# Expert rows through slot tables in DRAM in place of one-hot matmuls

## What is computed

```python
def moe_swiglu(x, router_w, router_b, w_gate_up, w_down):
    logits = x @ router_w + router_b                  # 256 tokens, 8 experts
    top_v, top_i = lax.top_k(logits, 2)
    gates = softmax(top_v)
    combine = sum(gates * one_hot(top_i))
    y = 0
    for e in range(8):                                # d_ff of an expert: 3584
        y = y + combine[:, e] * swiglu(x, w_gate_up[e], w_down[e])
    return y
```

## Time and profile before

| | us |
|---|---|
| median of 3 runs (2133.47 to 2137.73) | 2133.87 |
| profiled execution, first to last instruction | 2123.7 |
| TensorE matmul busy | 1955.9 (92%) |
| VectorE busy | 1397.3 (66%) |
| ScalarE busy | 1145.9 (54%) |
| GpSimd busy | 58.8 (3%) |
| mean granted TensorE clock | 0.924 |

### The profile page before, as it was taken

The page is one execution under the profiler, slowest core; times in us unless marked ns, Lnnn a source line. Parts: engine busy times, 40 slices in busy tenths (PEclk is TensorE's granted clock), DMA queues, the critical chain, the costliest instruction groups (busy, mean ns, idle before and its releaser), DMA issues.

```text
span 2123.7 us, 25981 instructions
## 1 busy us (share of the span) xinstructions
PE 1955.9 (92%) x9673; PEld 1625.0 (77%) x9673; DVE 1397.3 (66%) x1154; ACT 1145.9 (54%) x1009; POOL 58.8 (3%) x81
## 2 busy tenths in 40 slices
PE   7967999898889998877899999999999999999997
PEld 6756997685569986676687888878788787788875
DVE  3444775432254455454787888878888787888874
ACT  4333554343434333332576776767677776677762
POOL 1230000200000000000000000000000000000000
PEclk9958999896679999957799999999999999999997
DMA  6603455440034554401598999999999999899980
GB/s 227 197 30 138 158 193 185 141 165 21 0 134 169 197 178 159 139 1 60 204 363 310 351 350 334 351 321 358 341 334 348 331 354 332 316 352 337 362 296 35
DMA packets 251586, 486.86 MB, mean 229 GB/s; under 512 B 14108, under 2 KB 19292, under 8 KB 251536
## 3 DMA queue, kind: packets, MB, share of 16 engines
q1 hardware_dynamic: 244976, 477.30, 63.8%
q0 software_dynamic: 6560, 8.91, 1.4%
HBM read 484.05 MB, written 1.05 MB: 228 GB/s over the span
## 4 chain that ended last, share of the span: by engine, by line
PE 60%; DVE 13%; DMA 12%; ACT 8%; issue 4%; DVEq 2%; ACTq 0%; SPq 0%; POOL 0%; POOLq 0%
DMA w_raw<-in_moe_w_down 8%; PE psum L1759 8%; PE psum L1761 7%; PE psum L1760 7%; DVE w_lo L834 7%; PE psum L1416 7%; PE psum L1417 7%; PE psum L1418 6%; ACT w_hi L512 5%; DMA w_raw<-in_moe_w_gate_up 4%; PE psum L1447 3%; PE psum L1434 2%; PE psum L1437 2%; PE psum L1436 2%; PE psum L1802 1%
## 5 line engine op out<-in xcount | busy, mean ns | idle before, releaser
L834 DVE TENSOR_TENSOR w_lo<-w_raw,w_hi 128x2048 fp32r<-128x2048 f32 (+2 forms) x475 | 1031.7, 2200 | 384.1 <-ACT w_hi L512 381.1
L512 ACT ACTIVATE w_hi<-w_raw 128x2048 fp32r<-128x2048 f32 (+2 forms) x475 | 863.8, 1842 | 269.4 <-DMA w_raw<-in_moe_w_gate_up 103.8
L1759 PE MATMUL psum<-w_hi,xg_hi 128*128 128x512 f32 x896 | 360.3, 402 | 1.3 <-DVE w_lo L834 0.8
L1761 PE MATMUL psum<-w_hi,xg_lo 128*128 128x512 f32 x896 | 354.9, 396 | 0.0
L1760 PE MATMUL psum<-w_lo,xg_hi 128*128 128x512 f32 x896 | 354.8, 396 | 0.0
L1434 PE MATMUL psum<-xt_hi,w_hi 128*128 128x256 f32 x704 | 198.6, 282 | 3.8 <-DVE w_lo L834 2.1
L1761 PEld LDWEIGHTS psum<-w_hi,xg_lo 128*128 128x128 f32 x896 | 168.7, 188 | 41.0
L1759 PEld LDWEIGHTS psum<-w_hi,xg_hi 128*128 128x128 f32 x896 | 169.0, 189 | 40.2 <-DVE w_lo L834 1.7
L1760 PEld LDWEIGHTS psum<-w_lo,xg_hi 128*128 128x128 f32 x896 | 169.1, 189 | 38.0
L1436 PE MATMUL psum<-xt_lo,w_hi 128*128 128x256 f32 x704 | 197.9, 281 | 0.0
L1437 PE MATMUL psum<-xt_hi,w_lo 128*128 128x256 f32 x704 | 197.7, 281 | 0.0
(11 more groups left out here) (336 smaller groups left out, 2104.6 us busy)
## 6 DMA issues: line engine op xcount, KB each, us to landing
w_raw<-in_moe_w_gate_up SPq DMA_DIRECT2D x224, 1024.0 KB, 6.7
w_raw<-in_moe_w_down SPq DMA_DIRECT2D x96, 1024.0 KB, 6.7
w_raw<-in_w_up SPq DMA_DIRECT2D x22, 1024.0 KB, 5.7
w_raw<-in_ffn_w_gate_up SPq DMA_DIRECT2D x22, 1024.0 KB, 5.5
w_raw<-in_moe_w_down SPq DMA_DIRECT2D x32, 512.0 KB, 4.3
w_raw<-in_w_in SPq DMA_DIRECT2D x12, 1024.0 KB, 6.3
w_raw<-in_ab_w_in SPq DMA_DIRECT2D x12, 1024.0 KB, 5.4
w_raw<-in_w_down SPq DMA_DIRECT2D x10, 1024.0 KB, 6.5
```

The lines of the kernel that those rows point to most:

```text
L512: return act.activation(o, i, func, **kw)
L834: TT(w_lo[:, k % RING, 0:n], w_raw[:, k % RING, 0:n], w_hi[:, k % RING, 0:n].bitcast(F32), ALU.subtract)\
L1759: mm(o, hi[:, q, :], wh, start=(q == first), stop=False)
L1761: m = mm(o, lo[:, q, :], wh, start=False, stop=(q == last))
```

## The change

Tokens' rows go through tables in DRAM. At the start GpSimd fills x_slots (12 items of 128 rows) and the last three items of y_slots with zeros. After routing, each token has two slot numbers, one per chosen expert, and four indirect DMAs scatter the rows of x to x_slots. For each item SP loads its 128 rows (x_row), TensorE transposes them, and xg_hi and xg_lo are formed from that. The result is stored without the gate to y_slots by a DMA that ScalarE issues. At the end four indirect DMAs fetch each token's two rows, and VectorE adds them with the gates. The one-hot matmuls, sel, selt, xn_hi, xn_lo and ys_lo are gone.

```diff
+        (x_row, ys) = layout(at_xt, ("x_row", [P, D], F32), ("ys", [P, D], F32))
+        x_slots = nc.dram_tensor("x_slots", (ITEMS + 1, P, D), F32, kind="Internal").ap()
+        y_slots = nc.dram_tensor("y_slots", (ITEMS, P, D), F32, kind="Internal").ap()
# SP
+                def slot_rows(i):
+                    sp.wait_ge(S("x_scattered"), 16 * 2 * NT)
+                    sp.wait_ge(S("x_turned"), i)
+                    sp.dma_start(x_row[:], x_slots[bass.ds(i, 1)].rearrange("o p n -> (o p) n")).then_inc(S("x_row_landed"), 16)
...
+                        if j == MOE_PAIRS - 2:
+                            slot_rows(i + 1)
# GpSimd, after tri_ready
+                one(pool.memset(e2[:], 0.0))
+                for rows in [x_slots[i] for i in range(ITEMS + 1)] + [y_slots[i] for i in range(N_EXP, ITEMS)]:
+                    pool.dma_start(rows, e2[:].rearrange("p f n -> p (f n)")).then_inc(S("slots_zeroed"), 16)
# GpSimd, last
+                pool.wait_ge(S("slots_zeroed"), 16 * N_ZEROED)
+                pool.wait_ge(S("slot_ids"), 1)
+                for t in range(NT):
+                    for k in range(2):
+                        pool.indirect_dma_start(out=rows(x_slots), out_offset=row_of(t, k), in_=x[:, t, :], in_offset=None)\
+                            .then_inc(S("x_scattered"), 16)
+                pool.wait_ge(S("x_scattered"), 16 * 2 * NT)
+                pool.dma_start(x_row[:], x_slots[0]).then_inc(S("x_row0_landed"), 16)
+                pool.wait_ge(S("y_stored"), 1)
+                for t in range(NT):
+                    for k in range(2):
+                        pool.indirect_dma_start(out=y_row[:, t, k, :], out_offset=None, in_=rows(y_slots), in_offset=row_of(t, k))\
+                            .then_inc(S(f"y_landed{t}"), 16)
# ScalarE, start of the program, before the second exponential of cum
+            act.wait_ge(S("slots_zeroed"), 16 * N_ZEROED)
# ScalarE, end of an item (k is chunk 34 after take_item; 44 to 47 are the next item's 0 to 3)
+                rounds(k, k + 2, r)
+                take_item(i + 1)
+                k += 2
                 for n in range(2):
                     end = MOE_UP_CHUNKS + len(MOE_DOWN) * (n + 1)
                     rounds(k, end + 2, r)
                     k = end + 2
                     wait_used(act, c0 + end, r)
-                    copy(ys_hi[:, n * NB:(n + 1) * NB], psum[:, 4 + n, :], scale=gslot[:, 0:1])\
-                        .then_inc(S("ys_hi_ready"), 1)
-                take_item(i + 1, k, r)
+                    copy(ys[:, n * NB:(n + 1) * NB], psum[:, 4 + n, :]).then_inc(S("ys_ready"), 1)
+                act.wait_ge(S("ys_ready"), 2 * i + 4)
+                act.dma_start(y_slots[bass.ds(i, 1)].rearrange("o p n -> (o p) n"), ys[:]).then_inc(S("ys_landed"), 16)
+                rounds(k, k + 1, r)
+                act.wait_ge(S("ys_landed"), 16 * i + 16)
+                rounds(k + 1, k + 2, r)
# VectorE, end of an item
-                for n in range(2):
...
-                    STT(ys_lo[:, o], psum[:, 4 + n, :], gslot[:, 0:1], ys_hi[:, o].bitcast(F32), ALU.mult, ALU.subtract)\
-                        .then_inc(S("ys_ready"), 1)
+                splits(k, k + 2, r)
                 take_item(i + 1)
-                for t in range(NT):
-                    dve.wait_ge(S("scattered"), 2 * i + t + 1)
-                    TT(y[:, t, :], y[:, t, :], psum[:, 4 * t:4 * t + 2, :].rearrange("p b n -> p (b n)"), ALU.add)\
-                        .then_inc(S("y_added"), 1)
-                splits(k, k + 2, r)
+                splits(k + 2, MOE_CHUNKS + 4, r)
# VectorE, take_item
-                dve.tensor_copy(xg_lo[:], psum[:, 2:4, :].rearrange("p b (k n) -> p (b k) n", n=P)).then_inc(S("xg_ready"), 1)
+                dve.wait_ge(S("xg_hi_ready"), n + 1)
+                TT(xg_lo[:], psum[:, 2:4, :].rearrange("p b (k n) -> p (b k) n", n=P), xg_hi[:].bitcast(F32), ALU.subtract)\
+                    .then_inc(S("xg_ready"), 1)
# VectorE, after the last item
                 for t in range(NT):
+                    dve.wait_ge(S(f"y_landed{t}"), 32)
+                    for k, g in enumerate((g1, g2)):
+                        STT(y[:, t, :], y_row[:, t, k, :], g[:, t:t + 1], y[:, t, :], ALU.mult, ALU.add)
+                        dve.drain()
# TensorE
-            def gather(part, b0):
...
-            def turn_sel(n):
...
+            def turn_x(n):
+                for k in range(KD):
+                    m = turn(psum[:, 2 + k // 4, (k % 4) * P:(k % 4 + 1) * P], x_row[:, k * P:(k + 1) * P])
+                m.then_inc(S("x_turned"), 1)
...
                         if k == MOE_UP_CHUNKS:
                             turn_h(MOE_PAIRS - 1)
+                            pe.wait_ge(S("x_row_landed"), 16 * i + 16)
+                            turn_x(i + 1)
...
-                pe.wait_ge(S("sel_ready"), i + 2)
-                gather(xn_hi, 6)
-                gather(xn_lo, 2)
-                pe.wait_ge(S("ys_ready"), 2 * i + 2)
-                for t in range(NT):
-                    for n in range(2):
-                        for q, part in enumerate((ys_hi, ys_lo)):
-                            m = mm(psum[:, 4 * t + n, :], selt[:, t * P:(t + 1) * P], part[:, n * NB:(n + 1) * NB],
-                                   start=(q == 0), stop=(q == 1))
-                    m.then_inc(S("scattered"), 1)
-                turn_sel(i + 1)
# TensorE, before item 0
-                pe.wait_ge(S("sel_ready"), 1)
                 pe.wait_ge(S("ppt_ready"), 2)
-                gather(xn_hi, 6)
-                gather(xn_lo, 2)
-                turn_sel(0)
+                pe.wait_ge(S("x_row0_landed"), 16)
+                turn_x(0)
```

More of the change, by code:

```diff
@@ L766, in rounds, with take_item @@
                     round_chunk(N_BEFORE_MOE + k, r, item_width(k))
[L768 to L775, removed]
+            def take_item(n):
+                act.wait_ge(S("x_turned"), n + 1)
+                copy(xg_hi[:], psum[:, 2:4, :].rearrange("p b (k n) -> p (b k) n", n=P)).then_inc(S("xg_hi_ready"), 1)
             def item(i):
@@ L1326, in _ @@
                 dve.drain().then_inc(S("chosen"), 1)
+                dve.wait_ge(S("ranks"), 1)
+                ranks = scr[:, 1, 0:NT * N_EXP].rearrange("p (t e) -> p t e", e=N_EXP)
+                of_tiles = lambda v: v.unsqueeze(1).broadcast_to([P, NT, N_EXP])
+                TS(over, scr[:, 1, 16:24], float(P), None, ALU.is_gt)
+                TS(past, ranks, float(P), None, ALU.is_ge)
+                TT(slot_of, ranks, of_tiles(first8), ALU.add)
+                dve.drain()
+                dve.tensor_tensor_scan(over_upto, one8, over, 0.0, ALU.mult, ALU.add)
@@ new lines, in _ @@
+                dve.reduce_sum(eidf[:, 3:4], over, AX_X)
+                dve.drain()
+                STT(past8, over_upto, float(P), past8, ALU.mult, ALU.add)
+                TS(route_i[:, 3:4], eidf[:, 3:4], float(N_EXP), None, ALU.add).then_inc(S("counted"), 1)
+                dve.drain()
+                TT(past, past, of_tiles(past8), ALU.mult)
+                dve.drain()
+                TT(slot_of, slot_of, past, ALU.add)
+                dve.drain()
+                for k, (on, hot) in enumerate(((on1, hot1), (on2, hot2))):
+                    TT(on, slot_of, hot, ALU.mult)
@@ L1329, in _ @@
+                dve.drain()
+                for k, on in enumerate((on1, on2)):
+                    dve.reduce_sum(slotf[:, k, :], on, AX_X)
+                dve.drain()
+                dve.tensor_copy(slot_id[:], route[:, 228:232])
+                dve.drain().then_inc(S("slot_ids"), 1)
+                splits(2, 4, 0)
                 dve.wait_ge(S("top_exp"), 1)
-                dve.wait_ge(S("ranks"), 1)
-                sc, cc_ = (v.rearrange("p (t i) -> p t i", i=ITEMS) for v in (slotc[:, 0:NT * ITEMS], combc[:, 0:NT * ITEMS]))
@@ L1341, in _ @@
                 TT(g2, g1, gap_e, ALU.mult)
-                dve.tensor_tensor_scan(over_before, one8, over, 0.0, ALU.mult, ALU.add)
-                dve.reduce_sum(eidf[:, 3:4], over, AX_X)
-                dve.drain()
-                for hot, g in ((hot1, g1), (hot2, g2)):
-                    TT(hot, hot, g.unsqueeze(2).broadcast_to([P, NT, N_EXP]), ALU.mult)
-                dve.drain()
-                TT(comb, hot1, hot2, ALU.add)
-                TT(cc_[:, :, 0:N_EXP], hot1, hot2, ALU.add)
@@ L1351, in _ @@
-                dve.drain()
-                select(0)
-                TS(route_i[:, 3:4], eidf[:, 3:4], float(N_EXP), None, ALU.add).then_inc(S("counted"), 1)
-                TT(over_before, over_before, over, ALU.subtract)
-                take_item(0)
-                splits(2, 4, 0)
-                dve.drain()
                 for k in range(ITEMS - N_EXP):
-                    TS(pick, over_before, float(k), None, ALU.is_equal)
+                    TS(pick, tmp8, float(k), None, ALU.is_equal)
```

103 lines of the change are left out of this document (32 added, 71 removed).

## The result

| | before | after |
|---|---|---|
| median (us) | 2133.67 (2124.96 to 2137.73, 4 runs) | 2152.2 (2151.34 to 2152.84, 4 runs) |
| span of the profiled execution | 2123.7 | 2150.3 |
| after to before, all runs taken together, 95% interval | | 1.0096 [1.0068, 1.0123] |

The change made the kernel 18.5 us slower by the medians, 0.9%; the interval leaves out 1, so the loss is clear of the spread of the runs. The forecast was 2125 (2100 to 2150), faster: the sign was wrong and the time fell 2 us outside the range.

The account below looks back on a forecast made before the run. TensorE was taken to bound the inside of an item. Expert stage -23.8 us, ahead of item 0 +10.3 and behind the last item +4.5 gave -9.0, from 2133.9 to 2125 us (8-in-10 range 2100 to 2150).

Parts of the forecast that it names:

- the term for the boundary: Between two items: TensorE waits 0.8 us at chunk 0 and 1.3 before chunk 3, 2.1 per boundary (0.8 to 4.5).
- the lower clock ahead of item 0: Before the first expert matmul: eight transposes at the lower clock, 2.0 us; first matmuls 0.79 us in either kernel.
- The ring's term: Inside items: 1.05 MB more through the DMA engines costs 1.0 us per item (nothing to 2.7), 8 us in all.
- the stage: First to last expert matmul, eight items: 1032.8 us before, 1009.0 after, a change of -23.8 us.
- Ahead of item 0: Ranks to first expert matmul: slot numbers, four scatters, landing, x_row load, transposes; +10.3 us (+4 to +23).
- a sign of being wrong: Ahead of item 0: scatter issues above 2 us on GpSimd would show the forecast wrong; 1.2 us each was taken.
- Two covers of the prediction: Ahead of item 0: picking experts for second items is hidden under the scatters; without that cover some 6 us.
- Behind the last item: Last down matmul to statistics of y: store, indirect gathers and additions take 25.7 us against 21.2, +4.5 (-0.5 to +16).
- At the start: Fifteen zero writes (7.9 MB) on GpSimd's idle queue cost nothing; up to 20 us without that cover.
- The clean boundary: Rival: store lands in 2.8 us, each boundary costs 0.8, the ring takes the extra bytes; 2108 us, chance 0.20.
- The ring as the bound: Rival: the weight ring bounds the items, at 349 GB/s an item takes 129.2 us; total 2149 us, chance 0.16.
- The slow chain: Rival: GpSimd issues of 2.1 us and landings of 9.2, ahead of and behind the items; +15, 2149 us, chance 0.17.

Follow-up runs that it names:

- the moved wait: Changed kernel with ScalarE's wait for the ys store moved to just before the copy that overwrites ys, an item later: 2116.36 us, ratio 0.9937.
- the three runs on one chip: Changed kernel with the ys wait moved; without the ys store and wait; also without x_row loads for items 1 to 7: 2116.36, 2110.6, 2114.8 us.
- all kernels with a moved wait: Seven kernels on three chips with all the traffic and the ys wait moved an item later, some with further edits: items 125.1 to 126.3 us, mean 125.8.
- the three kernels of the first chip: Changed kernel with the ys wait moved; without the ys store and wait; also without x_row loads for items 1 to 7: ratios 0.9937, 0.9917, 0.993.
- the half store: Changed kernel, wait left in place, ys stored in two halves, each as soon as it is copied: 2145.07 us, ratio 1.0095.

## Why the prediction was wrong

**The step that failed is the term for the boundary: "With a landing time L ... It stalls L - 3.0 ... I take 4.3, since the store too shares the engines with two loads."** L is 7.0, above even the upper end of 6.7. With it the formula gives 4.0 + 0.8 = 4.8 us per boundary and the trace shows 4.6 (3.5 before chunk 3 and 1.1 before chunk 0). Mechanism and formula held; the size was taken from the nearest row by bytes (a 512 KB load between loads), when the nearest by position would have been the 6.7 us of the 1 MB loads that run with it. That is 2.5 us times seven, 18 us. Its bytes weren't the reason: the store's own packets take 2.7 us, and more than half of the landing passes before the first of them. The Trainium skill (DMA: Bandwidth & Descriptors, Anatomy of one DMA), cited in the prediction for 3.2 us, is further off; it gives the figure for transfers that GpSimd issues. The same section of the Trainium skill puts most of a transfer's fixed part into the receipt behind the last byte; these traces differ, with 3.6 to 4.1 us ahead of the first packet and 0.3 to 0.5 us between the last packet and the landing.

**What was not counted is the clock.** Windows of 10 us behind four stalls, and one across the start of an item:

```profile
1183.10:1193.10 10.00, 10.00 (x36) 7.94 (x37) 8.64 (x5) 6.85 (x4) 0.00 (x0) 0.83 0.85 290
...
1311.38:1321.38 10.00, 10.00 (x31) 7.99 (x32) 8.63 (x5) 6.85 (x4) 0.00 (x0) 0.70 0.83 288
...
1441.94:1451.94 10.00, 9.35 (x41) 7.33 (x42) 8.63 (x5) 7.16 (x5) 0.00 (x0) 1.00 0.83 282
...
1703.19:1713.19 10.00, 10.00 (x37) 7.96 (x38) 8.64 (x5) 6.86 (x4) 0.00 (x0) 0.84 0.86 292
...
1952.45:1962.40 9.95, 9.95 (x36) 7.72 (x36) 4.59 (x2) 3.97 (x4) 0.00 (x0) 0.84 1.01 360
```

Behind six of the seven stalls before chunk 3 the granted clock is 0.70 to 0.84: some matmuls stand 0.43 us apart (1.2 GHz) in place of 0.23. Against the moved wait this is 11.7 us over six items (747.70 - 735.98), 2.0 an item, 14 in seven. The prediction counted the lower clock ahead of item 0 only, though the window of 0.83 at 1800.19 us showed that a boundary can bring it.

**The ring's term isn't settled, and is small either way.** 18 + 14 us would be 32, and the stage missed by 27.6: the items are otherwise 0.6 us shorter than forecast. One microsecond an item for the extra bytes is 0.3 by the three runs on one chip and 1.0 against the mean of all kernels with a moved wait. With the wait out of the way an item takes 125.1 us, where the forecast's terms without the 2.1 at the boundary give 124.1; 2.5 us of idle time are left in it. The rule of the Trainium skill (DMA: Bandwidth & Descriptors, Specifications) of about 358 GB/s per core, weighed in the prediction, would have set 126, an estimate from that figure; here 360 GB/s held over 750 us and 388 over the 10 us from 1429.76, and the item without 1.05 MB of its traffic was hardly shorter, so no such limit decides it.

**Ahead of item 0**, +14.8 where +10.3 was forecast. The slot numbers cost 3.9 us from the last matmul of the ranks to the first scatter, 0.4 more than was said. The issues took 7.1 us in place of 4.8 (one of them 2.30, above the 2 us that the prediction named as a sign of being wrong), the landing 7.9 in place of 5.0, and issue and load of x_row together 3.7 in place of 4.9. Two covers of the prediction worked against it: it saw the expert choice hidden "under the scatters", but not that the splits beside it slow the indirect issues and that the reloads they set free share the DMA engines. An indirect issue that begins under a split ends somewhat less than one issue's length after the split does: the third begins at 1025.13, the splits end at 1026.14, it ends at 1026.98, 0.84 us later; behind the last item the first gather ends 0.87 us after the split under which it began (2095.05, 2095.92). The Trainium skill (SBUF — State Buffer, SBUF: two separate sides) has VectorE operations with two SBUF inputs lock GpSimd out of a shared port while it reads SBUF, which fits the indirect issues (slot_id lies in SBUF) and the plain ones at 0.53 us under the same split; the runs show the coincidence, not the port.

**Behind the last item**, +6.1 where +4.5 was forecast. The ys copy came 4.2 us after the last matmul, since ScalarE's order puts two roundings before it that had waited 7.0 us for PLE's weights; and GpSimd's first indirect issue took 2.94 us. Leaving the loop gave 2 us back: 0.3 in place of 2.4. The store landed in 4.8 us here, near the forecast's 4.3.

**At the start** nothing, as said: the 8 MB of zeros cost no time that the marks of the first stages show; the +1.8 up to the ranks isn't explained and is no more than these stages vary: the last matmul of the ranks begins anywhere from 1014.1 to 1018.9 us in the experiments.

**The rivals.** The clean boundary (2108) comes nearest to the kernel without this wait, but isn't reached: 2108 is 0.988 of the 2133.87 that it started from, and the three kernels of the first chip have 0.992 to 0.994, with items of 125 us where it named 123.7. The ring as the bound gave 2149 and named an item of 129.2 us; the time came out near it by another mechanism, so the number was right and the rival wrong. The slow chain, also 2149, is there in part (+21 of its +39 us). The chance of 0.64 for faster rested on one term between 0.8 and 4.5 us, seven times over; its upper end alone put the sum at 2142.

**Still open:** what holds a store's first packet back for 3.6 to 4.1 us beside the loads, and what spreads the items of the kernels with the moved wait over 1.2 us.

## What to carry to other kernels

When an engine that feeds the bound one issues a transfer, ask where the wait for its landing stands, and put it at the next use of the buffer, not behind the next instruction: this one edit is worth 36 us here (2152.0 to 2116.4 us on one chip, the first with two splits moved as well, which changed nothing in the ratio to the kernel before, 1.0096 either way) and turns 0.9% slower into 0.6% faster. Size an unseen landing beside running streams by the longest transfer that runs with it, not by one of equal bytes: here that would have said 6.7 for the 7.0. And ahead of a chain that the core waits for, look at what frees ring slots and starts loads: two splits moved by 16 us made the chain 7 us shorter.

## What the runs showed of the hardware that was not expected

- A 512 KB store on ScalarE's queue, issued beside SP's running weight loads, lands in 7.0 us, one of 256 KB in 6.3; with idle engines 512 KB land in 2.75. What differs most is the time to the first packet: 3.6 to 4.1 us against 0.9.
- The idle time of TensorE alone doesn't tell whether its clock falls: after 2.26 us at 1952.45 the next matmul took 0.79 us, after 3.44 us at 1441.94 it took 0.50 and the clock stayed at 1.00. With the half store it fell to 0.83 behind a stall of 2.23 us and stayed at 1.00 behind three of 2.34 to 2.72.
- An indirect DMA of 128 rows takes GpSimd 0.94 to 1.06 us to issue, and 1.85 to 2.9 where it begins under a VectorE split.
- The last of the four scatters lands 3.3 us behind its issue without the reloads and 7.9 with 2 MB of them beside it.
